# Forgetting attention: odd query tiles hold their low halves on top, and the second score products of two tiles contract 64 partitions each

## The reference, cut to what matters

```python
def forgetting_attention(q, k, v, log_f, key_valid):
    ...
    cum = jnp.swapaxes(jnp.cumsum(log_f, axis=1), 1, 2)
    ...
    for i in range(lp // Q_BLOCK):
        lo, hi = i * Q_BLOCK, (i + 1) * Q_BLOCK
        s = jnp.einsum('bqhd,bkhd->bhqk', q[:, lo:hi], k[:, :hi]).astype(jnp.float32) * (HEAD_DIM ** -0.5)
        s = s + cum[:, :, lo:hi, None] - cum[:, :, None, :hi]
        mask = (idx[None, :hi] <= idx[lo:hi, None]) & key_valid[None, :hi]
        p = jax.nn.softmax(jnp.where(mask, s, -jnp.inf), axis=-1)
        outs.append(jnp.einsum('bhqk,bkhd->bqhd', p.astype(v.dtype), v[:, :hi]))
```

## Time and profile before

| | |
|---|---|
| median of 3 runs | 2385.95 us (2384.6 to 2387.75) |
| the profiled execution | 2384.95 us |
| its span, first to last instruction | 2383.3 us |
| forgetting attention in it | from 658 to 1167 us |
| TensorE busy, of the span | 2156.1 us (90%) |
| mean granted TensorE clock | 0.952 |

### The profile page before, as it was taken

The page is one execution under the profiler, slowest core; times in us unless marked ns, Lnnn a source line. Parts: engine busy times, 40 slices in busy tenths (PEclk is TensorE's granted clock), DMA queues, the critical chain, the costliest instruction groups (busy, mean ns, idle before and its releaser), DMA issues. The chain is left out here.

```text
span 2383.3 us, 35822 instructions
## 1 busy us (share of the span) xinstructions
PE 2156.1 (90%) x11168; PEld 1771.5 (74%) x11168; DVE 1652.9 (69%) x3067; ACT 1485.1 (62%) x2262; POOL 489.1 (21%) x561
## 2 busy tenths in 40 slices
PE   6999999969889999999899984999999999999980
PEld 5788888745567777777688873878888888788860
DVE  4323332167588888888633346999999999999976
ACT  4323241276577777777533332878888888878867
POOL 0111110143122222322000001122222222222221
PEclk9999999979989999999899996999999999999995
DMA  6435352543432222222233324997987969999838
GB/s 204 165 123 182 116 177 81 167 94 92 103 103 63 72 70 72 72 63 81 72 124 141 141 97 178 360 375 237 297 265 229 296 204 361 326 304 299 265 91 300
DMA packets 220554, 420.60 MB, mean 176 GB/s; under 512 B 47913, under 2 KB 97145, under 8 KB 219289
## 3 DMA queue, kind: packets, MB, share of 16 engines
q1 hardware_dynamic: 187760, 316.08, 39.5%
q0 software_dynamic: 31648, 101.89, 14.9%
q10 hardware_dynamic: 1040, 1.31, 0.2%
HBM read 437.68 MB, written 86.39 MB: 220 GB/s over the span
## 5 line engine op out<-in xcount | busy, mean ns | idle before, releaser
L2537 DVE TENSOR_TENSOR moe_w_lo<-fetch_w_raw,moe_w_hi 128x1024 fp32r<-128x1024 f32 x376 | 435.3, 1218 | 8.8 <-ACT moe_w_hi L2466 8.7
L2466 ACT ACTIVATE moe_w_hi<-fetch_w_raw 128x1024 fp32r<-128x1024 f32 x376 | 368.5, 1052 | 62.3 <-DMA fetch_w_raw<-in_w_e_up_dram 30.3
L2591 PE MATMUL moe_ps_gu<-moe_w_hi,moe_xT_hi 128*128 128x512 f32 x736 | 293.0, 398 | 4.0 <-DVE moe_xT_lo L2548 4.0
L2593 PE MATMUL moe_ps_gu<-moe_w_hi,moe_xT_lo 128*128 128x512 f32 x736 | 288.6, 392 | 0.0
L2592 PE MATMUL moe_ps_gu<-moe_w_lo,moe_xT_hi 128*128 128x512 f32 x736 | 288.5, 392 | 0.0
L1569 DVE TENSOR_TENSOR fox_p_lo<-fox_ps_t,fox_p_hi 128x512 fp32r<-128x512 f32 (+4 forms) x352 | 211.4, 612 | 46.6 <-ACT fox_p_hi L1502 44.8
L1502 ACT ACTIVATE fox_p_hi<-fox_ps_t 128x512 fp32r<-128x512 f32 (+4 forms) x352 | 182.0, 533 | 84.3 <-PE fox_ps_t L1640 83.5
L2543 DVE TENSOR_TENSOR moe_d_lo<-fetch_d_raw,moe_d_hi 128x1024 fp32r<-128x1024 f32 x184 | 213.1, 1220 | 11.0 <-ACT moe_d_hi L2474 8.2
L1640 PE MATMUL fox_ps_t<-ident,fox_s 128*128 128x128 f32 (+1 forms) x1216 | 197.8, 277 | 21.7 <-ACT fox_s L1495 21.5
L1556 DVE CUSTOM_DVE_ANT_0 fox_s<-fox_ps_r,fox_ncum 128x512 f32<-128x512 f32 (+4 forms) x352 | 191.3, 568 | 16.7 <-PE fox_ps_r L1625 9.6
L511 ACT ACTIVATE proj_qk_out<-proj_ps_chunk 128x512 f32<-128x512 f32 x52 | 31.1, 598 | 261.7 <-PE proj_ps_chunk L744 261.7
(11 more groups left out here) (346 smaller groups left out, 5153.3 us busy)
## 6 DMA issues: line engine op xcount, KB each, us to landing
fetch_w_raw<-in_w_e_gate_dram SPq DMA_DIRECT2D x192, 512.0 KB
fetch_w_raw<-in_w_e_up_dram SPq DMA_DIRECT2D x192, 512.0 KB
fetch_d_raw<-in_w_e_down_dram SPq DMA_DIRECT2D x92, 1024.0 KB
ahead_raw<-in_w_in_dram SPq DMA_DIRECT2D x24, 1024.0 KB, 5.3
gates_wide<-in_x_dram SPq DMA_DIRECT2D x16, 512.0 KB
h<-gates_wide POOLq DMA_DIRECT2D x16, 512.0 KB, 3.3
gates_wide<-qT SPq DMA_DIRECT2D x32, 256.0 KB, 4.4
mix_h<-h SPq DMA_DIRECT2D x16, 512.0 KB, 3.7
```

The source lines that it names most:

```text
L2466: nc.scalar.activation(w_hi[:, k], w_raw[:, k].rearrange("p j n -> p (j n)"), ACT.Copy).then_inc(gu_high, 1)
L2537: nc.vector.tensor_tensor(w_lo[:, k], w_raw[:, k].rearrange("p j n -> p (j n)"), w_hi[:, k].bitcast(F32), ALU.subtract).then_inc(gu_split, 1)
L2591: nc.tensor.matmul(out, xT_hi[:, slot, k], w_hi[:, k, cols], start=k == 0, stop=False)
L2593: done = nc.tensor.matmul(out, xT_lo[:, slot, k], w_hi[:, k, cols], start=False, stop=k == KT - 1)
```

## The change

In odd tiles `q_two` now holds the low part on top, in partitions 0 to 63, and the high part below. Score rows of two tiles (0 and 1, 2 and 3 of a unit) alternate, and `partner` pairs those of the same chunk. Of a pair TensorE does both products with `k_hi` and both masks first. Then come the two products with `k_lo`, each over the 64 partitions in which its tile has the high part; the product of low queries and low keys is left out in these. An odd tile's last chunk that has no partner keeps the product over 128 partitions. The low split of 512 query columns becomes two instructions, one for the even and one for the odd tiles, of 2 x 128 columns each; `q_split` counts twice.

```diff
@@ -1263,13 +1263,22 @@
         rows, pieces, blocks = [], [], []
         rows_before, pieces_before, blocks_before = [0], [0], [0]
         for n, (h, g) in enumerate(units):
-            rows += [(n, j, c, key, width) for j in range(4) for c, (key, width) in enumerate(row_chunks(4 * g + j))]
+            rows += [(n, j, c, key, width) for even in (0, 2) for c in range(len(row_chunks(4 * g + even + 1)))
+                     for j in (even, even + 1) for key, width in row_chunks(4 * g + j)[c:c + 1]]
             pieces += [(n, j, c, key, width) for j in range(4) for c, (key, width) in enumerate(row_pieces(4 * g + j))]
             blocks.append((n, TILES, META, 0))
             blocks += [(n, b, P, P * max(0, b - 4 * g)) for b in range(4 * g + 4)]
             rows_before.append(len(rows))
             pieces_before.append(len(pieces))
             blocks_before.append(len(blocks))
+        partner = {}
+        for r in range(len(rows) - 1):
+            n, j, c = rows[r][0:3]
+            if j % 2 == 0:
+                assert rows[r + 1][0:3] == (n, j + 1, c)
+                partner[r], partner[r + 1] = r + 1, r
+        rows_to = {(n, j): max(r for r, row in enumerate(rows) if row[0:2] == (n, j)) + 1
+                   for n in range(UNITS) for j in range(4)}
         copy_at = {blocks_before[n + 1] + LAG: n for n in range(UNITS - 1)}
         back_at = {blocks_before[n + 1] + LAG + 1: n for n in range(UNITS - 1)}
         row_at = [[sum(P * (4 * g + i + 1) + META for i in range(j)) for j in range(5)] for g in range(GROUPS4)]
@@ -1328,6 +1337,16 @@
 
         K_COLS = [slice(0, FIRST)] + [slice(SBT * i + META, SBT * (i + 1) + META) for i in range(1, PIECES)]
         Q_COLS = [slice(SBT * i, SBT * (i + 1)) for i in range(PIECES)]
+
+        def low_queries(u, i, odd):
+
+            half = slice(0, HD) if odd else slice(HD, P)
+
+            def tiles_of(columns):
+                return columns.rearrange("p (a b n) -> p a b n", b=2, n=P)[:, :, odd]
+
+            return tiles_of(q_two[half, u, Q_COLS[i]]), tiles_of(q_raw[half, Q_COLS[i]])
+
         V_ROWS = [slice(0, 8), slice(8, BLOCKS)]
         SPLITS = [("v", 0), ("k", 0), ("q", 0), ("v", 1)] + [(what, i) for i in range(1, PIECES) for what in "kq"]
 
@@ -1339,12 +1358,11 @@
             for n in range(-1, UNITS):
                 events = []
                 if n + 1 < UNITS:
-                    g = units[n + 1][1]
                     ahead = range(rows_before[n + 1], rows_before[n + 2])
                     rate = SPREAD / len(ahead)
-                    events += [(rate * (i + 0.5), "scores", r) for i, r in enumerate(ahead)]
+                    events += [(rate * (max(r, partner.get(r, r)) - ahead[0] + 0.5), "scores", r) for r in ahead]
                     for j in range(4):
-                        done = sum(len(row_chunks(4 * g + i)) for i in range(j + 1))
+                        done = max(rows_to[n + 1, j], partner.get(rows_to[n + 1, j] - 1, 0) + 1) - rows_before[n + 1]
                         events.append((rate * (done + 0.4), "tops", 4 * (n + 1) + j))
                         mine = [r for r in range(pieces_before[n + 1], pieces_before[n + 2]) if pieces[r][1] == j]
                         events += [(rate * (done + 0.8) + 0.14 * SPREAD * (i + 0.5) / len(mine), "exp", r)
@@ -1396,14 +1414,14 @@
                 sp.wait_ge(k_split, PIECES * h)
                 load_keys(h, slice(0, FIRST), 0)
                 load_keys(h, slice(FIRST, TOK), 1)
-                sp.wait_ge(q_split, PIECES * h)
+                sp.wait_ge(q_split, 2 * PIECES * h)
                 load_queries(h, slice(0, SBT), 0)
                 load_queries(h, slice(SBT, SEQ), 1)
                 if h >= 2:
                     sp.wait_ge(biased, rows_before[GROUPS4 * (h - 1)])
                 sp.dma_start(ncum[:, h % 2], row_broadcast(t["ncum"][h], P)).then_inc(cum_in[h % 2], 16)
             sp.wait_ge(k_split, PIECES * B_HEADS)
-            sp.wait_ge(q_split, PIECES * B_HEADS)
+            sp.wait_ge(q_split, 2 * PIECES * B_HEADS)
             sp.wait_ge(v_split, 2 * B_HEADS)
             for k in range(KT):
                 sp.dma_start(w_piece(ahead, k), t["w_o"][0, k * P:(k + 1) * P, :]).then_inc(ahead["w_in"][k], 16)
@@ -1425,7 +1443,7 @@
                 for sem, count in latest.items():
                     pool.wait_ge({"k": k_split, "q": q_split, "v": v_split}[sem], count)
                 latest.clear()
-                latest[what] = (2 if what == "v" else PIECES) * h + i + 1
+                latest[what] = {"v": 2 * h + i + 1, "k": PIECES * h + i + 1, "q": 2 * (PIECES * h + i + 1)}[what]
                 if what == "k":
                     pool.wait_ge(k_high, PIECES * h + i + 1)
                     pool.wait_ge(k_split, PIECES * h + i)
@@ -1433,9 +1451,10 @@
                                             ALU.subtract).then_inc(k_split, 1)
                 elif what == "q":
                     pool.wait_ge(q_high, PIECES * h + i + 1)
-                    pool.wait_ge(q_split, PIECES * h + i)
-                    nc.gpsimd.tensor_tensor(q_two[HD:P, u, Q_COLS[i]], q_raw[HD:P, Q_COLS[i]],
-                                            q_two[HD:P, u, Q_COLS[i]].bitcast(F32), ALU.subtract).then_inc(q_split, 1)
+                    for odd in range(2):
+                        pool.wait_ge(q_split, 2 * (PIECES * h + i) + odd)
+                        low, raw = low_queries(u, i, odd)
+                        nc.gpsimd.tensor_tensor(low, raw, low.bitcast(F32), ALU.subtract).then_inc(q_split, 1)
                 else:
                     pool.wait_ge(v_high, 2 * h + i + 1)
                     pool.wait_ge(v_split, 2 * h + i)
@@ -1534,8 +1553,9 @@
                                             ALU.subtract).then_inc(k_split, 1)
                 elif what == "q":
                     dve.wait_ge(q_high, PIECES * h + i + 1)
-                    nc.vector.tensor_tensor(q_two[HD:P, u, Q_COLS[i]], q_raw[HD:P, Q_COLS[i]],
-                                            q_two[HD:P, u, Q_COLS[i]].bitcast(F32), ALU.subtract).then_inc(q_split, 1)
+                    for odd in range(2):
+                        low, raw = low_queries(u, i, odd)
+                        nc.vector.tensor_tensor(low, raw, low.bitcast(F32), ALU.subtract).then_inc(q_split, 1)
                 else:
                     dve.wait_ge(v_high, 2 * h + i + 1)
                     nc.vector.tensor_tensor(v_two[:, u, V_ROWS[i], HD:2 * HD], v_raw[:, V_ROWS[i]],
@@ -1560,7 +1580,7 @@
             def tops(which):
                 n, j = which // 4, which % 4
                 g = units[n][1]
-                dve.wait_ge(biased, rows_before[n] + sum(len(row_chunks(4 * g + i)) for i in range(j + 1)))
+                dve.wait_ge(biased, rows_to[n, j])
                 nc.vector.tensor_reduce(ntop[:, n % 2, j:j + 1], mx[g][:, j], AX.X, ALU.max, negate=True).then_inc(maxed, 1)
 
             def probabilities_low(k):
@@ -1611,22 +1631,37 @@
                     pe.wait_ge(biased if what == "row" else folded, which + 1)
                 return ps_r[place % R_BANKS]
 
-            def scores(r):
+            def score_parts(r):
                 n, j, c, key, width = rows[r]
                 h, g = units[n]
-                i, u = 4 * g + j, h % 2
+                i = 4 * g + j
+                return (ps_r[ring_of["row", r] % R_BANKS], h % 2, slice(i * P, (i + 1) * P), slice(key, key + width), width,
+                        key + width == P * (i + 1) + META)
+
+            def high_scores(r):
+                n, j, c, key, width = rows[r]
+                h, g = units[n]
                 if j == 0 and c == 0:
                     pe.wait_ge(k_split, PIECES * h + g + 1)
-                    pe.wait_ge(q_split, PIECES * h + g + 1)
-                bank = score_bank(("row", r))
-                out, queries, keys = bank[:, 0:width], slice(i * P, (i + 1) * P), slice(key, key + width)
-                last = key + width == P * (i + 1) + META
-                nc.tensor.matmul(out, q_two[:, u, queries], k_hi[:, u, keys], start=True, stop=False)
-                done = nc.tensor.matmul(out, q_two[:, u, queries], k_lo[:, u, keys], start=False, stop=not last)
+                    pe.wait_ge(q_split, 2 * (PIECES * h + g + 1))
+                score_bank(("row", r))
+                bank, u, queries, keys, width, last = score_parts(r)
+                nc.tensor.matmul(bank[:, 0:width], q_two[:, u, queries], k_hi[:, u, keys], start=True, stop=False)
                 if last:
-                    done = nc.tensor.matmul(bank[:, width - P:width], ident_r[:], future_r[:],
-                                            start=False, stop=True)
-                done.then_inc(rows_done, 1)
+                    nc.tensor.matmul(bank[:, width - P:width], ident_r[:], future_r[:], start=False, stop=False)
+
+            def low_scores(r, half):
+                bank, u, queries, keys, width, last = score_parts(r)
```

(10 more changed lines are left out.)

## The result

The changed kernel takes 2491.38 us (median of 4 runs, 2487.73 to 2494.23) against 2386.85 us before: 1.0438 times as long, with a 95% interval of 1.042 to 1.0456. That is 104.5 us slower. The forecast was slower by 59 us, and its range ended at 2486 us.

The account below looks back on a forecast made before the run. TensorE and VectorE were taken as level in the forgetting attention's dense part, added TensorE time counting in full; slots -31, switches +59, late exponentials +22, banks +3, clock +6 gave +59 us, 2445 us, range 2380 to 2486.

Parts of the forecast that it names:

- The sign: Whole kernel: slower by 59 us; slower by over 0.2% had chance 0.80, within 0.2% 0.06, faster 0.14.
- the late exponentials: ScalarE at unit ends: waits longer by 1.5, 1.1 and 0.1 us for fourth, third and second units; +22 us.
- the clock: TensorE after the other long wait: one more clock fall per head, up to 1.6 us, half taken; +6 us.
- The slots and the switch: TensorE's dense part: side-by-side halves save 31 us of slots; 160 contraction-height changes and returns at 0.37 us add 59.
- the rival in which the halves don't run side by side: TensorE's pairs: no slot saved, switches and other costs stay; 2476 us, chance 0.15.
- The 16-partition value matmuls: TensorE's matmuls over 16 meta keys, taken as nearest evidence for the switch price: 0.37 us per pair.
- The score banks: Three score banks: once per head a second pair waits 0.4 us for a bank being read; +3 us.
- At nothing: Low query split as two GpSimd instructions: cost hidden by GpSimd's idle time, below 0.3 us a piece without that cover.
- The stretches: Forgetting attention: the 16.1 us stretch becomes near 19 us, the 22.4 us one changes by under 1 us.

Follow-up runs that it names:

- alternation: Kernel before with the rows of two tiles alternating, each made whole, tops and exponentials behind their own tile's last row: 2412.32 us, 1.0109.
- places in the lists: Kernel with alternating rows, each made whole, but both rows of a pair at the second's place and exponentials as much later: 2458.51 us, against 2412.32.
- 2458.5: Kernel with alternating whole rows, both rows of a pair at the second's place, low products over 128 partitions: 2458.51 us, 1.0301 times the kernel before.
- the late exponentials alone: Kernel before with only the first and third tile's exponentials moved in ScalarE's list to where the second's and fourth's stand: 2426.93 us, 1.0162.
- the pair of runs 46 us apart: Kernel before with alternating whole rows, 2412.32 us; the same with both rows of a pair at the second's place and exponentials later, 2458.51 us.
- the first-place runs: Changed kernel with pairs at their first row's place, exponentials behind their own tile's last row: 2451.2 us with halves, 2423.95 us over 128 partitions.
- without its seven falls: Kernel before with 12 useless matmuls in the one wait per head after which its clock falls: 2370.16 us, 0.9931.
- Filling the waits: Changed kernel with 4 to 15 useless matmuls before the waiting transposes at a unit's end: 2471.33 us, 1.0344 times the kernel before.
- the run with the halves alone: Kernel before, row order kept and nothing paired, with each low product over the 64 partitions of its tile's high part: 2516.51 us, 1.0551.

## Why the prediction went wrong

The sign was right, the size was not: 104.5 us against 59, past the range's end by 5 us. Two terms of the sum were too small, that of the late exponentials and, more so, that of the clock. The steps in turn, with the single tests adding up as +26 (alternation), +46 (places in the lists) and +33 (halves, 2491.4 less 2458.5).

*The slots and the switch* (-31 + 59 = +28) held in mechanism, and the number came out well in part by luck. The halves run side by side, a change costs up to 0.2 us each way, and a round takes 1.96 us where 1.97 was forecast. The halves cost 27 to 33 us, but only 16 to 22 of it is TensorE's own time; the rest is the clock, which the forecast did not put here. So the rival in which the halves don't run side by side fell, though its 2476 us stood nearer to the result than the forecast did. The 16-partition value matmuls (0.37 us) were a fair row to go by: 0.38 us for a row behind a row, 0.31 in the mean. The rule of the Trainium skill, "TensorEngine Tiling (Array Packing)", Key Properties, that a change of tiling mode drains the engine, agrees with the timeline above for 64 rows as well. The rule of the Trainium skill, "TensorE: Matmul & The Clock Gate", Part 3, that row-tiled matmuls overlap, agrees too: the two halves' records together last 0.50 us, one alone 0.49. The overlap saves less than the changes of height cost.

*The late exponentials* (+22) is the first step that failed, in size. The mechanism is shown, by the late exponentials alone, by the pair of runs 46 us apart whose lists differ by one row's place, and by the first-place runs. The size was short: the wait at the fourth unit's end grew from 0.88 to 2.55 us, 1.7 where 1.5 was forecast, but at the third it grew by 2.0 and not by 1.1, and at the second by 0.8 and not by 0.1. I worked out the fourth unit from ScalarE's list and scaled the third by the length of its pieces. I did not lay out its list. There ScalarE first idles 2.46 us, so the delay is not absorbed. At the second unit I took the 1.00 us of ScalarE's idle time as cover, but two waits now stand there in place of one. In sum 4.5 us a head, 36 us; the other 4 of the waits' +40 are the stage's first wait, 6.5 us where it was 2.4. So this term was short by 14 to 18 us.

*The clock* (+6) is the second step that failed, and the larger one. It was sized for one more fall per head and at 0.8 us. There are two more per head: one behind each of the three waits. A fall costs more as well: without its seven falls the kernel before is 18 us faster, some 2.5 us for each. And the stage begins with a longer time at the lower level, 31 us up to the first unit's output where it was 17. In all it has 62 us more at the lower level, some 31 us by the estimate above, 25 more than the term had. Filling the waits gave back 20 us in the changed kernel. The forecast had a reader look for a fall behind the fourth unit's wait, and it is there, 0.60 in the 4 us from 954:

```profile
954.00:958.00 4.00, 3.69 (x16) 3.16 (x17) 2.55 (x5) 2.72 (x8) 1.45 (x2) 0.60 0.96 231
```

*The score banks* (+3): the wait for them grew by 3 us, as forecast. The idle time in front of value matmuls, which no term had, grew by 6 us. *At nothing*: the low split in two instructions shows nowhere in TensorE's waits, as forecast. *The stretches*: 16.1 us became 20.5, not 19; the one of 13.4 became 18.4, for which I had given no figure, and it lost the most; that of 22.4 us grew by 1.2 and not by under 1.

What stays open: why the clock stays low for 30 us and more of busy time in the run with the halves alone, and why the halves lengthen the time at the lower level at the start of the stage. That half of the time at the lower level is lost is an estimate, borne out by two runs and not measured for each.

## What to carry to other kernels

Two matmuls over half of the partitions do run side by side, but going to half height and back costs 0.31 to 0.38 us here, more than the 0.23 us slot of 512 columns that is saved. By these numbers it would pay only with two or more such pairs per change, which no run here tried. When rows of two tiles are interleaved, ask first when each tile is complete, and lay out the waiting engine's list for every unit rather than scale it from one. An idle wait on TensorE may cost more behind it than in it (1.4 us of wait and some 2.5 us behind it in the kernel before): look at the granted clock after each wait, and add up the time at the lower level over the stage, before calling the wait the whole price.

## What the runs showed of the hardware that was not expected

Twelve matmuls without use in a wait of 1.4 us per head made the kernel 0.7% faster (2370.16 against 2387.98 us), with the clock at 1.00 behind the wait where it was 0.59. And in the run with the halves alone the granted clock was 0.52 for 32 us, and 0.51 for 44 us, during which TensorE was busy without a gap, so there being busy by the record was not enough to have it at its upper level.
